# Two decoder layers on one core: the scale of a pair of tiles from a GpSimd reduce over partitions

## What is computed

```python
def peer_ffn(x, w_q, sub_keys, u_tab, v_tab):      # x: 256 tokens by 1024
    q = (x @ w_q).reshape(B, S, PEER_HEADS, 2, PEER_HALF)
    s = einsum('bshcd,hckd->bshck', q, sub_keys)
    # top 16 of each half, top 16 of their sums -> experts e, gates g
    h = gelu(einsum('bcd,bced->bce', x, u_tab[e]))
    return einsum('bce,bced->bcd', g * h, v_tab[e])

x = layer_norm(ALPHA * x + mixer(x))
x = layer_norm(ALPHA * x + peer_ffn(x, ...))
```

## Time and profile before

| | |
|---|---|
| median of 3 runs | 1773.82 us (1772.23 to 1774.85) |
| the profiled execution, its time | 1772.14 us |
| its span | 1770.1 us |
| mean granted TensorE clock | 0.999 of full speed |
| busy: TensorE, VectorE, ScalarE, GpSimd | 1753.4, 1470.5, 1328.2, 459.7 us |
| HBM read | 328.20 MB |

### The profile page before, as it was taken

One profiled execution on the slowest core, in us unless ns is written; L12 is line 12 of the kernel. 1 busy time (PEld: TensorE's weight loads), 2 busy tenths in 40 slices (PEclk: granted clock), 3 DMA queues, 4 the chain that ended last, 5 costly groups with the idle time before them and its releaser, 6 DMA issues.

```text
span 1770.1 us, 37869 instructions
## 1 busy us (share of the span) xinstructions
PE 1753.4 (99%) x14056; PEld 1377.9 (78%) x14056; DVE 1470.5 (83%) x2604; ACT 1328.2 (75%) x1777; POOL 459.7 (26%) x643
## 2 busy tenths in 40 slices
PE   8999999999999999999999999999999999999998
PEld 8779888999988888544487898889999888884443
DVE  8878988788878888788898799897777788877887
ACT  4689999888864445888746899998888644468885
POOL 0010001122223333555400100111222233335553
PEclk9999999999999999999999999999999999999999
DMA  8456655555545566666274555555555355756660
GB/s 261 155 203 203 200 196 184 198 184 186 182 131 179 178 233 230 228 200 202 84 219 139 213 203 201 199 185 192 184 180 190 129 178 169 270 193 239 203 203 33
DMA packets 96004, 333.51 MB, mean 188 GB/s; under 512 B 11680, under 2 KB 16032, under 8 KB 95648
## 3 DMA queue, kind: packets, MB, share of 16 engines
q1 hardware_dynamic: 88992, 317.51, 52.5%
q10 hardware_dynamic: 6912, 14.77, 2.7%
HBM read 328.20 MB, written 4.03 MB: 188 GB/s over the span
## 4 chain that ended last, share of the span: by engine, by line
PE 93%; DVE 4%; ACT 2%; issue 1%; POOL 0%; DVEq 0%; ACTq 0%; POOLq 0%
PE bank L1811 14%; PE bank L1813 13%; PE bank L1812 13%; PE bank L1862 9%; PE bank L1864 9%; PE bank L1863 9%; PE bank L1878 6%; PE bank L1880 6%; PE bank L1882 6%; PE bank L2140 3%; DVE half_tiles L1129 1%; PE bank L1950 1%; PE bank L2097 1%; ACT squares_unread L711 1%; DVE matched_keys L1573 0%
## 5 line engine op out<-in xcount | busy, mean ns | idle before, releaser
L1811 PE MATMUL bank<-xt_half,half_tiles 128*128 128x256 f16 x2272 | 618.9, 272 | 2.3 <-DVE half_tiles L1129 1.3
L1813 PE MATMUL bank<-xt_half,half_tiles 128*128 128x256 f16 x2272 | 619.1, 273 | 0.0
L1812 PE MATMUL bank<-xt_half,half_tiles 128*128 128x256 f16 x2272 | 619.0, 272 | 0.0
L1129 DVE SCALAR_TENSOR_TENSOR half_tiles<-raw,to_half,half_tiles 128x1024 f16<-128x1024 f32 x280 | 357.4, 1277 | 88.6 <-ACT half_tiles L703 87.3
L693 ACT ACTIVATE hi<-raw 128x1024 fp32r<-128x1024 f32 x184 | 194.5, 1060 | 238.1 <-PE bank L1864 203.1
L703 ACT ACTIVATE half_tiles<-raw,to_half 128x1024 f16<-128x1024 f32 x280 | 319.3, 1140 | 6.5 <-POOL to_half L609 6.2
L711 ACT ACTIVATE squares_unread<-raw 128x2048 bf16<-128x2048 f32 x140 | 266.3, 1902 | 0.6 <-DMA raw<-in_stream 0.4
L1811 PEld LDWEIGHTS bank<-xt_half,half_tiles 128*128 128x128 f16 x2272 | 222.1, 98 | 28.7 <-issue 2.8
L1112 DVE TENSOR_TENSOR lo<-raw,hi 128x1024 fp32r<-128x1024 f32 x184 | 240.3, 1308 | 4.5 <-ACT hi L693 3.1
L1813 PEld LDWEIGHTS bank<-xt_half,half_tiles 128*128 128x128 f16 x2272 | 222.1, 98 | 25.9
L1812 PEld LDWEIGHTS bank<-xt_half,half_tiles 128*128 128x128 f16 x2272 | 222.0, 98 | 24.1
(11 more groups left out here) (256 smaller groups left out, 2781.5 us busy)
## 6 DMA issues: line engine op xcount, KB each, us to landing
raw<-in_stream SPq DMA_DIRECT2D x464, 512.0 KB, 3.7
v_raw<-in_stream SPq DMA_DIRECT2D x128, 512.0 KB, 4.2
early_raw<-in_stream SPq DMA_DIRECT2D x8, 512.0 KB, 6.1
shifted_u<-x_kept ACTq DMA_DIRECT2D x16, 142.0 KB, 5.3
ln_g<-in_ln_p ACTq DMA_DIRECT2D x4, 512.0 KB, 6.5
ln_b<-in_ln_p ACTq DMA_DIRECT2D x4, 512.0 KB, 8.0
keys_sb<-in_keys_t ACTq DMA_DIRECT2D x2, 1024.0 KB, 6.5
x_kept<-x ACTq DMA_DIRECT2D x4, 512.0 KB, 4.3
```

The source lines that it names most:

```text
L1129: vec.scalar_tensor_tensor(here[:, 1, :], raw_of(f), to_half[:, slot:slot + 1], here[:, 0, :], ALU.mult, ALU.subtract)\
L1811: mm(dst, weight(0, slot, k), xt[:, k, 0, :], start=k == 0, stop=False)
L1812: mm(dst, weight(0, slot, k), xt[:, k, 1, :], start=False, stop=False)
L1813: last = mm(dst, weight(1, slot, k), xt[:, k, 0, :], start=False, stop=k == KC - 1)
```

## The change

GpSimd finds the scale of a unit alone. `partition_all_reduce` with `max` takes the largest of the 128 partitions' sums of squares into all partitions of `peaks`; a TENSOR_SCALAR reads it as a whole number, multiplies by 2^-24 and stores a rounded whole number, half the exponent, into `bound`, now int32 with one column per unit; `to_half` and `from_half` are made from that, with constants 2^13 away from those before. The step for unit 0 stands ahead of the last three steps of the scale of x. TensorE's `unit_sum`, VectorE's `bound_of` and all calls of them go, with the waits of TensorE for `bound_made`.

```diff
             for layer in range(DEPTH):
+                def unit_scale(q):
+                    column = slice(q % 2, q % 2 + 1)
+                    slot = slice(q % UNIT_SLOTS, q % UNIT_SLOTS + 1)
+                    pool.wait_ge(*squared(layer, q + 1))
+                    nc.gpsimd.partition_all_reduce(peaks[:, column], squares[:, column], P,
+                                                   bass.bass_isa.ReduceOp.max).then_inc(*peak_made.one)
+                    pool.wait_ge(*peak_made(layer, q + 1))
+                    nc.gpsimd.tensor_scalar(bound[:, q:q + 1], whole_number(peaks[:, column]),
+                                            2.0 ** -12, 2.0 ** -12, ALU.mult, ALU.mult)\
+                      .then_inc(*bound_made.one)
+                    pool.wait_ge(*bound_made(layer, q + 1))
+                    nc.gpsimd.tensor_scalar(whole_number(to_half[:, slot]), bound[:, q:q + 1],
+                                            -float(1 << 23), float(204 << 23), ALU.mult, ALU.add)\
+                      .then_inc(*unit_made.one)
+                def unit_back(q):
+                    slot = slice(q % UNIT_SLOTS, q % UNIT_SLOTS + 1)
+                    nc.gpsimd.tensor_scalar(whole_number(from_half[:, slot]), bound[:, q:q + 1],
+                                            float(1 << 23), x_peak[:, 7:8], ALU.mult, ALU.add)\
+                      .then_inc(*back_made.one)
...
+                unit_scale(0)
                 pool.wait_ge(*x_power(layer, 1))
...
-                for q in range(UNITS):
-                    slot = slice(q % UNIT_SLOTS, q % UNIT_SLOTS + 1)
-                    pool.wait_ge(*bound_made(layer, q + 1))
...
+                unit_back(0)
+                for q in range(1, UNITS):
+                    unit_scale(q)
+                    unit_back(q)
...
-                def bound_of(q):
-                    dve.wait_ge(*summed_ps(layer, q + 1))
...
-                    if f % 2 == 0 and 2 <= f // 2 + 1 < UNITS:
-                        bound_of(f // 2 + 1)
...
-                def unit_sum(first, turn=0):
-                    pe.wait_ge(*squared(layer, 2 * turn + (first + 1)))
-                    if first > 2:
-                        pe.wait_ge(*bound_made(layer, 2 * turn + first))
-                    upper = squares[:, first % 2:first % 2 + 1].bitcast(bf16)[:, 1:2]
-                    mm(unit_bank(first), sums_of[:, :], upper, start=True, stop=True)\
-                      .then_inc(*summed_ps.one)
```

More of the change, by code:

```diff
@@ L213, in build @@
         sums_of = place("bound_sums", [P, P], bf16)
-        bound = place("unit_bound", [P, UNITS])
+        bound = place("unit_bound", [P, UNITS], mybir.dt.int32)
+        peaks = place("unit_peaks", [P, 8])
         to_half = place("to_half", [P, UNIT_SLOTS])
@@ L353, in build @@
         early_in = [signal(f"early_raw_in{q}", 2, 16) for q in range(EARLY // 2)]
-        squared, summed_ps = signal("unit_squared", UNITS), signal("unit_sum_ps", UNITS)
-        bound_made = signal("unit_bound_made", UNITS)
+        squared = signal("unit_squared", UNITS)
+        bound_made, peak_made = signal("unit_bound_made", UNITS), signal("unit_peak_made", UNITS)
         unit_made, back_made = signal("unit_made", UNITS), signal("unit_back_made", UNITS)
@@ L453, in v_sum_bank @@
             return bank[7 if g == 0 or g % 2 else 3][:, 0:1]
-        def unit_bank(q):
-            return bank[5 if q == 0 else 2 if q == 1 else 3][:, SEQ + q % 2:SEQ + q % 2 + 1]
         def unit_loads(q):
@@ L603, in _ @@
                 nc.gpsimd.tensor_scalar(x_peak[:, 7:8], whole_number(x_peak[:, 6:7]),
-                                        float(-63 << 23), None, ALU.add).then_inc(*x_unit.one)
+                                        float(-76 << 23), None, ALU.add).then_inc(*x_unit.one)
                 pool.wait_ge(*x_unit(layer, 5))
-                for q in range(UNITS):
-                    slot = slice(q % UNIT_SLOTS, q % UNIT_SLOTS + 1)
-                    pool.wait_ge(*bound_made(layer, q + 1))
[L609 to L614, removed]
+                unit_back(0)
+                for q in range(1, UNITS):
+                    unit_scale(q)
+                    unit_back(q)
                 pool.wait_ge(*reach_made(layer, 1))
                 nc.gpsimd.tensor_scalar(w_unit[:, 3:4], whole_number(w_unit[:, 1:2]), -1.0,
-                                        float(309 << 23), ALU.mult, ALU.add).then_inc(*w_made.one)
+                                        float(322 << 23), ALU.mult, ALU.add).then_inc(*w_made.one)
                 pool.wait_ge(*u_top(layer, 1))
                 pool.wait_ge(*w_made(layer, 2))
-                nc.gpsimd.tensor_scalar(w_unit[:, 4:5], whole_number(w_unit[:, 2:3]), -1.0,
+                nc.gpsimd.tensor_scalar(w_unit[:, 4:5], w_unit[:, 2:3], -float(1 << 23),
                                         w_unit[:, 3:4], ALU.mult, ALU.add).then_inc(*w_made.one)
@@ L1447, in _ @@
                                   EXPONENT, None, ALU.bitwise_and).then_inc(*x_power.one)
-                bound_of(0)
                 layer_norm(0, ln1_g, ln1_b, x1_ready)
-                bound_of(1)
                 x_rests(4)
@@ L1819, in half_tile, with first_by_x @@
                     tile_by_x(slot, dst, half_weight, xt_half)
-                def first_by_x(n0, dsts, done, ready, clock_products, weight=weight, xt=xt,
-                               between=None):
+                def first_by_x(n0, dsts, done, ready, clock_products, weight=weight, xt=xt):
                     tiles = list(enumerate(dsts, n0))
@@ L1829, in first_by_x @@
                             transpose_x(ready(t, c), t, c)
-                        if between and t == 0:
-                            between()
                     for c in range(2):
@@ L2081, in attention_ready @@
                     pe.wait_ge(*mix_lo(layer, c + 1))
-                    if c == RING - 1:
-                        unit_sum(0)
                     pe.wait_ge(*lo_done[n % RING](layer, n // RING + 1))
@@ L2100, in key_scores @@
                         last.then_inc(*sp_ps.one)
-                pe.wait_ge(*bound_made(layer, 1))
                 first_by_x(WQ0, [acc_banks[e][:, 0:SEQ] for e in range(2)], 4,
                            lambda t, c: x1_ready(layer, 2 * t + c + 1), AT_NORM, half_weight,
-                           xt_half, lambda: unit_sum(1))
-                unit_sum(2)
+                           xt_half)
                 for n in range(WQ0 + 2, U0):
                     pe.wait_ge(*lo_done[n % RING](layer, n // RING + 1))
-                    if n == WQ0 + 2:
-                        pe.wait_ge(*bound_made(layer, 2))
                     if n >= WQ0 + QP_BANKS:
@@ L2113, in _ @@
                     half_tile(n % RING, acc_banks[(n - WQ0) % QP_BANKS][:, 0:SEQ])
[L2114 to L2117, removed]
                     if n > WQ0 and (n - WQ0) % TOP_GROUPS == 0:
@@ L2123, in u_ready, with u_tile @@
                     pe.wait_ge(*lo_done[j](layer, i + (U0 // RING + 1)))
-                def u_tile(i, j, sums=2):
+                def u_tile(i, j):
                     u_ready(i, j)
@@ L2128, in u_tile @@
                     half_tile(j, ring_banks[j][:, 0:SEQ])
-                    if j % 2 and j // 2 < sums:
-                        unit_sum((U0 - WQ0 + j + 5) // 2, i)
                 def gate_matrices(seg, i, k, slot=0):
@@ L2164, in _, with gates_beside @@
                         u_tile(i, j)
-                def gates_beside(i, sums):
+                def gates_beside(i):
                     for j in range(RING):
@@ L2170, in gates_beside @@
                                 gate_matrices(0, i, j // GROUP_TILES + slot, slot)
[L2171 to L2175, removed]
+                        u_tile(i + G_TURN, j)
+                with pe.Fori(0, TURNS - G_TURN - 1) as i:
+                    gates_beside(i)
                 for j in range(RING):
@@ L2178, in _ @@
                         gate_matrices(0, TURNS - G_TURN - 1, j // GROUP_TILES)
-                    u_tile(LAST, j, 0)
+                    u_tile(LAST, j)
                 def v_part(j):
```

## The result

The changed kernel takes **3084.64 us** (median of 6 runs, 3081.2 to 3089.53), the kernel before 1772.84 in the same runs: ratio 1.740, 95% interval 1.739 to 1.742. The forecast was 3130, range 2320 to 4310. The profiled execution has a span of 3087.1 us.

What follows compares the result with a forecast made beforehand. TensorE bounded the kernel before; GpSimd was to take over the stage. Per unit 2 x 6.5 + 0.5 + 1.37 + 0.2 = 15.1 us, against 5.63; 1772.1 + 2 x 678.3 = 3128.8, so 3130 us, range 2320 to 4310.

Steps and rivals of the forecast that it cites:

- The reload: GpSimd's library switch, two per unit in the U stage: 6.5 us each, ends 3.7 and 10.6.
- The reduce: GpSimd's reduce over 128 partitions of one column, once per unit: 0.5 us, between 0.19 and 1.27.
- The three small steps: Three TENSOR_SCALAR per unit on GpSimd: new one and `to_half` at 0.43, `from_half` at 0.51, 1.37 us in all.
- The stage's new length: 72 units of 15.1 us plus a tail move the V stage's start from 524.63 to 1203, 678.3 us a layer.
- the tail behind unit 71: Two heads, two rests and two TensorE tiles between the last unit's scale and the V stage: about 8 us.
- Nothing hides it: In the U stage GpSimd always finds its next square done, so its 15.1 us a unit run without pause.
- the clock costs nothing: At 1.2 GHz TensorE would need 10.6 us a unit, still inside GpSimd's 15.1.
- TensorE's gain is worth nothing here: Removing 144 one-column products, 37 us at most, gains nothing because TensorE idles behind GpSimd.
- Rival A: The switch is cheap (reload under 1.8 us) and hidden on GpSimd; kernel gets faster, 1740 us; chance 0.13.
- The 0.26 us of a product: Extra time of each one-column product in TensorE's stream, 0.37 where 0.11 would do; times 144, 37 us at most.
- The chance of 0.09 for faster: The part of the cheap-switch rival's 0.13 in which the whole kernel gains over 0.2%.
- More instruction traffic: A sign that the forecast is right: DMA would show more instruction traffic; no size given.

Runs made afterwards that it cites:

- its own run: The changed kernel with 30 extra products of 256 columns behind each U tile on TensorE, into a bank nobody reads: 3083.14 us, ratio 1.739.
- the run with two units a stay: The changed kernel with one switch to library 1 and back (a stay) for two units, reduce and small steps on two columns: 2224.95 us, ratio 1.255.

## Why the prediction was right

- **The reload** (the term that decides): taken at 6.5 from the landing of `ln_g`, measured 5.9 into library 1 and 7.7 back, 13.6 for both against 13.0. The Trainium skill, page GPSIMD Engine Reference, section Instruction dispatch, has about 6 us for loading code; into library 1 this case's trace agrees with 5.9, and back it is 7.7. The page ties the price to the first call behind the load. The run with loads alone paid as much although nothing called library 1, and for library 1 the measurement decides; for library 0 no run here can tell. That there are 288 reloads was read from the order, not from the diff, and is the step that carries the forecast. That the size came out so close is in part luck. It was borrowed from a transfer, and no run shows that a library arrives by one like it. And the row was one of several: `ln_b`, which goes to all partitions as `ln_g` does, took longer than the 6.5 that the prediction gives as the longest transfer into the core, and by its 8.0 the same sum gives about 3560 us.

```profile
ln_b<-in_ln_p ACTq DMA_DIRECT2D x4, 512.0 KB, 8.0
```

- **The reduce**: 0.5 taken, 0.44 measured, and only 0.10 to 0.14 more for a second one.
- **The three small steps**: 1.37 taken from their means before, 0.64 measured. At 0.19 they now all run at the shortest duration that the earlier trace rows show, 0.26 for `from_half`; the means before had held-up steps in them, and with VectorE busy for 48% of the span and no longer 83% these are gone. That VectorE holds them up is a guess; what speaks for it is that the reduce, 0.44 on average here, takes 0.64 and 0.66 in the two kernels where the steps are on VectorE and it is busy for 85%. The 0.73 too much here and the 0.6 too little for the reloads nearly cancel, which is luck too: period 14.71 against 15.1.
- **The stage's new length**: the V stage starts at 1181.4 for a forecast 1203, a difference of 656.8 us a layer for 678.3. Of the 21.5, 72 x 0.39 = 28 are the period; the other way go 3 for the tail behind unit 71, 1170.3 to 1181.4, 11 us for 8, and 3.5 for unit 0, whose two loads took 7.4 and 9.8.
- **Nothing hides it; the clock costs nothing; TensorE's gain is worth nothing here**: as forecast, the clock with its own run. Between the V stage's first product and layer 1's unit 0 it is 1181.42 to 1661.69 = 480 us for 477.5 forecast.
- **Rival A** fell on its first premise: a load of the library that is there is no switch. Its price was wrong too. The 0.26 us of a product, 37 us in sum, came from one row that had a pause in it; the average is 0.044 and taking all of them off gives 2.4 us. With the switches out of the way the kernel ended within 0.2% of before (1772.41, the run with the library loaded ahead), not at 1740. The chance of 0.09 for faster was too high for that reason.
- **More instruction traffic** was expected in the DMA and is not there: the two instruction queues moved 0.80 and 0.45 MB, before 0.84 and 0.40. The run with loads alone (288 switches) and the one with 288 loads of the resident library have the same bytes in every queue, 0.84 and 0.44 MB in these two. So the loads of libraries do not appear in the queues that the profile lists, and what a switch spends its 5.9 or 7.7 us on stays open.

## What to carry to other kernels

## What the runs showed of the hardware

- In the changed kernel a library switch on GpSimd takes 5.7 to 7.4 us into library 1 (median 5.9) and 6.9 to 10.2 back into library 0 (median 7.7), the longest at the start of the stage. It has no row of its own: it is idle time put down to "issue", or lies inside a wait that ends later (the 8.08 us of the run with two units a stay).
- The same load with the library already there costs the kernel nothing: 288 of them, ratio 1.000 (0.999 to 1.001).
- The price of library 1 does not need a call of its code: 13.7 us for the two loads with nothing between, as much as with a reduce there.
- A reduce over 128 partitions of one column takes 0.38 us at its shortest and 0.44 on average in the changed kernel, 0.35 and 0.64 where VectorE is busy for 85%; a second one right behind it adds 0.10 to 0.14 us.
